# Two blocks of a model on one core: feed-forward up-projections as 512-column matmuls, and a second operator in GpSimd's multiplications

## The chip, the cores and the metric

The kernel runs on one core of a Trainium2 chip. The core has TensorE (PE in the rows, its weight loads PEld), VectorE (DVE), ScalarE (ACT), GpSimd (POOL) and SyncE (SP, which here issues every DMA). The metric is the time of one execution on the device, in microseconds (us); less is better.

## The reference

Two blocks are computed one after the other, for one sequence of 256 tokens of width 2048, all in fp32. The first has a modulation by c, a mixer (a recurrence and a pooling part) and a feed-forward with a convolution over three tokens; the second has another modulation and two attention branches. The change touches the feed-forward and the modulation:

```python
c_act = jax.nn.silu(c)
mod = c_act @ w_ada[l] + b_ada[l]          # w_ada: 2048 x 12288; the second block has its own, 2048 x 6144
...
def _conv_ffn(h, w_up, conv_w, conv_b, w_down):
    u = h @ w_up                           # 2048 -> 2 x 5632 features
    up = jnp.pad(u, ((0, 0), (CONV_WIDTH - 1, 0), (0, 0)))
    y = conv_b
    for j in range(CONV_WIDTH):
        y = y + conv_w[j] * up[:, j:j + T]
    val, gate = jnp.split(y, 2, axis=-1)
    return (jax.nn.silu(gate) * val) @ w_down
```

## The kernel before

Activations lie with features on the 128 partitions and the 256 tokens along the free dimension. Products are made to nearly fp32 from parts of fewer bits: every operand is split into a high and a low part, and three products are summed: weight high by activation high, weight high by activation low, weight low by activation high. The activations' parts of one feature tile lie side by side in `ACTS`, `AH` being the high 256 columns and `AL` the low 256.

Work comes in **units** of 1 MB of weights. For each unit SP loads the weights into one of four ring slots (`ring`), ACT copies them to the high part (`w_high`, L1337), DVE subtracts to get the low part (`w_low`, L1737), and PE multiplies. The order of units is fixed in a list, each engine runs its own written-out order, and semaphores join them. A slot is loaded again when PE has finished its unit; ACT and DVE split two units ahead.

There are two ways in which PE does a unit of 16 feature tiles. `std` makes, for each tile, two matmuls of 256 columns with the high weights into the same 256 columns of a PSUM bank (L768, L769), then 16 of 256 columns with the low weights (L772). `paired` makes one matmul of 512 columns with the high weights, over `AH` and `AL` together, into the 512 columns of the bank (L785), then the 16 with the low weights into the first half (L788). After `paired` the two halves of the bank must still be added: ACT copies the first half to SBUF and DVE adds the second half to it (`added`, L1847) and frees the bank. After `std` ACT's copy is the whole result and frees the bank.

The **feed-forward** goes through the 5632 hidden features in 11 turns of 512. Turn i has 8 up units (4 value tiles and 4 gate tiles, in turn) and then the 4 down units of the turn before it, `down(i - 1, s)`; before the change all 88 up units are done with the columns of `std` (the first three by `tiled`, tile by tile as the input becomes ready). For each up unit ACT copies the bank to `rawu` (L1539) and DVE convolves it in `conv` (L2163 to L2165); for each pair DVE multiplies gate and value (`hfu`, L2170), ACT makes the high part, and DVE the low part (`hid_low`, L2175). In a down unit DVE adds both of its banks to the running sum `dacc` (L2200). DVE's order is: split the weights of the unit two ahead, then the work on this unit; after the eighth up unit come the four down units, again each with a split ahead of it.

**GpSimd** makes part of the modulation, c times `w_ada`, beside the rest. In `quarters` a turn of 512 columns of `w_ada` comes in four quarters; for each of 16 tiles GpSimd multiplies by a column of `cact` (L623 for the first, else L625) and adds to a running sum (L626), each instruction waiting for the one before. Two turns (`acc_e`) are made at the start of the program, eleven (`acc2`) beside the eleven turns of the feed-forward, and four more (`acc_g`, L689 and L693) during the attention. PE takes up the sum of turn i - 1 at the end of turn i. SP's queue loads the quarters between the rings' weights: a quarter waits until GpSimd has finished the second last one (`f_free`, L452), and the loads behind it in the queue wait with it.

Of the kernel before, what the change touches and what calls it, by code (L numbers as in the profile page):

```python
# [17 lines left out]
ALU = mybir.AluOpType  # L18
# [3 lines left out]
T = 256  # L22
D = 2048
DT = D // P
# [105 lines left out]
def program(nc, xT_in, consts, att_consts, params, pos, w_ada, w_in, w2, a2, g2, pool_w, w_out, w_up, w_down,  # L130
            w_ada2, w_in2, w_kvb, w_mla, w_dil, w_o, out):
    ctx = ExitStack()
    with ctx:
# [469 lines left out]
        def _(pool):  # L603
# [11 lines left out]
            def quarters(k, acc, prod, first):  # L615

                for q in range(4):
                    pool.wait_ge(f_landed[k % 2], 16 * (k // 2 + 1))
                    w = (AE if k < 4 * N_FIRST else AF)[k % 2][:, :].rearrange("p (j n) -> p j n", j=4)
                    for j in range(4):  # L620
                        col = cact[:, first + 4 * q + j:first + 4 * q + j + 1]
                        if q == j == 0:
                            ins = pool.tensor_scalar(acc[:, :], w[:, j, :], col, None, ALU.mult)  # L623
                        else:
                            after(pool.tensor_scalar(prod[:, :], w[:, j, :], col, None, ALU.mult))  # L625
                            ins = pool.tensor_tensor(acc[:, :], prod[:, :], acc[:, :], ALU.add)  # L626
                        if j < 3:
                            after(ins)
                    k += 1
                    ins.then_inc(f_free, 1)  # L630
                    pool.wait_ge(f_free, k)
                pool.memset(small[:, 56:57], 0.0).then_inc(ada_sums, 1)
# [48 lines left out]
            for turn in range(N_LATE):  # L681
                acc = acc_g[turn % 2]
                if turn >= 2:
                    pool.wait_ge(ada_full, N_EARLY + 1 + N_FFN + turn - 1)
                for j in range(DT):
                    k = DT * turn + j
                    pool.wait_ge(g_landed[k % 2], 16 * (k // 2 + 1))
                    o = acc if j == 0 else prod_g[:, :].rearrange("p (a b) -> p a b", a=2)
                    pool.tensor_scalar(o, AG[k % 2][:, :].rearrange("p (a b) -> p a b", a=2), cact[:, DT + j:DT + j + 1], None,  # L689
                                       ALU.mult).then_inc(g_free, 1)  # L690
                    pool.wait_ge(g_free, k + 1)
                    if j:
                        after(pool.tensor_tensor(acc, o, acc, ALU.add))  # L693
                pool.memset(small[:, 56:57], 0.0).then_inc(ada_sums, 1)
# [10 lines left out]
        def _(pe):  # L705
# [452 lines left out]
            for i in range(12):  # L1158
                if i == 0:
                    tiled([("up", 0, k) for k in range(3)], 0)  # L1160
                    std(("up", 0, 3), 3)
                elif i < 11:
                    for k in range(4):
                        std(("up", i, k), k)
                if i < 11:
                    for k in range(4, 8):
                        std(("up", i, k), k % 4)
                if i:
                    for s in range(4):
                        down(i - 1, s)  # L1170
                    ada(acc2[(i - 1) % 2])
# [158 lines left out]
        def _(act):  # L1330
# [199 lines left out]
            for i in range(12):  # L1530
                for k in range(8):
# [4 lines left out]
                    if i < 11:  # L1536
                        unit("up", i, k)
                        act.wait_ge(raw_free, B.up("raw_free"))
                        act.activation(rawu[k % 2][:, 2:T + 2], bank[k % 4][:, 0:T], ACT.Copy)\  # L1539
                            .then_inc(bank_free[k % 4], 1)  # L1540
                    if k % 2 == 0 and (k or i):
                        finish()
                    if k == 7 and 0 < i < 10:
# [180 lines left out]
        def _(v):  # L1724
# [430 lines left out]
            ahead("up", 0, 3, to=0)  # L2155

            def conv(i, n):
                raw_tile(n % 4)
                u = rawu[n % 2]
                gate = n % 2  # L2160
                o = sil[:, :] if gate else cva[n // 2 % 2][:, :]
                k = 4 * i + n // 2 + 44 * gate
# [412 lines left out]
```

## Time and profile before

| | |
|---|---|
| time, median of 3 runs | 2772.86 us (2759.91 to 2775.61) |
| span of the profiled execution | 2768.1 us |
| busy: PE, PEld | 2643.3 us (95%), 2397.8 us (87%) |
| busy: DVE, ACT, POOL | 1864.0 (67%), 1082.6 (39%), 1128.9 us (41%) |
| chain that ended last | PE 80%, DMA 6%, POOL 6%, DVE 5% |

The span runs from the first to the last instruction of the profiled execution; its time as a run is not listed apart from that, and the median of the runs lies 4.8 us above the span. A busy share is a mean over stages with different limits, and PE's busy time is modelled: the end of a matmul overlaps the next one, so PE's pace is read from the distance between starts. The feed-forward runs from about 700 us to about 1475 us of the span.

### The profile page before, as it was taken

The numbers are of one execution on the slowest core, as the hardware profiler recorded it, in microseconds if no ns is written. First come the engines' busy times: TensorE is split into PE (matmuls) and PEld (weight loads), VectorE is DVE, ScalarE is ACT, GpSimd is POOL, SyncE is SP. The second block draws the span as 40 slices with busy tenths as digits, with TensorE's granted clock in tenths as the row PEclk, the third lists the DMA queues.
The fourth block names the chain that finished last, engine by engine and source line by source line (L and its number), as shares of the span: only waits on it lengthen the run. The fifth ranks groups of instructions, "written<-read, shape, count | busy, mean of one in ns | idle before, by whom it ended". The sixth has DMA issues, their size and how long they took to land.

```text
span 2768.1 us, 47948 instructions
## 1 busy us (share of the span) xinstructions
PE 2643.3 (95%) x20992; PEld 2397.8 (87%) x20992; DVE 1864.0 (67%) x2268; ACT 1082.6 (39%) x1255; POOL 1128.9 (41%) x612
## 2 busy tenths in 40 slices
PE   5689989999999999999999999999999999999997
PEld 2268877778999999999999899989988898999996
DVE  1248863267988888888887775576446874786454
ACT  1133422144434444343446443444334444444353
POOL 0293011013899999999991475862000000000001
PEclk7689989899999999999999999999999999999998
DMA  8967647676877777777765776775767665666664
GB/s 314 321 180 187 183 153 256 221 230 191 228 218 240 240 240 240 240 243 244 243 221 138 190 194 201 209 209 171 183 193 187 161 174 179 172 168 168 183 185 120
DMA packets 759185, 568.49 MB, mean 205 GB/s; under 512 B 46497, under 2 KB 645665, under 8 KB 758849
## 3 DMA queue, kind: packets, MB, share of 16 engines
q1 hardware_dynamic: 758976, 565.42, 69.7%
q8 instruction: 166, 2.72, 0.4%
q14 instruction: 43, 0.34, 0.0%
HBM read 563.29 MB, written 2.10 MB: 204 GB/s over the span
## 4 chain that ended last, share of the span: by engine, by line
PE 80%; DMA 6%; POOL 6%; DVE 5%; ACT 1%; issue 1%; SPq 1%; DVEq 0%; POOLq 0%
PE bank L785 15%; PE bank L768 9%; PE bank L769 9%; PE bank L772 9%; PE bank L788 8%; PE bank L752 5%; PE bank L754 5%; PE bank L753 5%; PE bank L1009 2%; DMA ada<-w_ada 2%; PE bank L741 2%; PE bank L821 2%; PE bank L822 2%; PE bank L823 2%; POOL prod_e L625 1%; POOL prod L625 1%
## 5 line engine op out<-in xcount | busy, mean ns | idle before, releaser
L1737 DVE TENSOR_TENSOR w_low<-ring,w_high 128x2048 fp32r<-128x2048 f32 x388 | 951.2, 2452 | 341.9 <-ACT w_high L1337 334.8
L1337 ACT ACTIVATE w_high<-ring 128x2048 fp32r<-128x2048 f32 x388 | 738.5, 1904 | 368.7 <-DMA ring<-w_in 127.6
L768 PE MATMUL bank<-acts,w_high 128*128 128x256 f32 x2400 | 586.4, 285 | 0.0
L769 PE MATMUL bank<-acts,w_high 128*128 128x256 f32 x2400 | 583.6, 283 | 0.0
L785 PE MATMUL bank<-acts,w_high 128*128 128x512 f32 (+1 forms) x2064 | 502.3, 396 | 11.1 <-DVE acts L1804 6.4
L768 PEld LDWEIGHTS bank<-acts,w_high 128*128 128x128 f32 x2400 | 461.6, 192 | 1.1 <-issue 0.2
L769 PEld LDWEIGHTS bank<-acts,w_high 128*128 128x128 f32 x2400 | 461.7, 192 | 0.0
L785 PEld LDWEIGHTS bank<-acts,w_high 128*128 128x128 f32 (+1 forms) x2064 | 382.7, 190 | 89.9 <-DVE acts L1804 6.5
L625 POOL TENSOR_SCALAR prod<-adf,cact 128x512 f32<-128x512 f32 x165 | 378.8, 2296 | 22.2 <-DMA adf<-w_ada 6.1
L639 POOL TENSOR_TENSOR sumf<-sqf 128x256 f32<-128x256 f32 x1 | 0.7, 743 | 789.7 <-ACT sqf L1718 789.7
L772 PE MATMUL bank<-acts,w_low 128*128 128x256 f32 x2400 | 312.4, 283 | 0.0
L626 POOL TENSOR_TENSOR acc<-prod,acc 128x512 f32<-128x512 f32 x165 | 299.0, 1812 | 13.8
L772 PEld LDWEIGHTS bank<-acts,w_low 128*128 128x128 f32 x2400 | 298.8, 192 | 0.0
L788 PEld LDWEIGHTS bank<-acts,w_low 128*128 128x128 f32 (+1 forms) x2064 | 264.1, 191 | 12.6 <-DVE w_low L1737 2.5
L788 PE MATMUL bank<-acts,w_low 128*128 128x256 f32 (+1 forms) x2064 | 268.0, 283 | 1.3 <-DVE w_low L1737 1.3
L752 PE MATMUL bank<-hid_high,w_high 128*128 128x256 f32 x704 | 201.0, 285 | 6.7 <-DVE dacc L2202 3.4
L754 PE MATMUL bank<-hid_high,w_low 128*128 128x256 f32 x704 | 200.7, 285 | 0.0
L753 PE MATMUL bank<-hid_low,w_high 128*128 128x256 f32 x704 | 200.5, 285 | 0.0
L689 POOL TENSOR_SCALAR prod_g<-adg,cact 128x512 f32<-128x512 f32 x60 | 117.0, 1951 | 92.3 <-DMA adg<-w_ada 89.2
L752 PEld LDWEIGHTS bank<-hid_high,w_high 128*128 128x128 f32 x704 | 136.7, 194 | 7.3 <-issue 4.4
L753 PEld LDWEIGHTS bank<-hid_low,w_high 128*128 128x128 f32 x704 | 136.6, 194 | 0.0
L754 PEld LDWEIGHTS bank<-hid_high,w_low 128*128 128x128 f32 x704 | 136.5, 194 | 0.0
(457 smaller groups left out, 3711.2 us busy)
## 6 DMA issues: line engine op xcount, KB each, us to landing
ring<-w_in SPq DMA_DIRECT2D x182, 1024.0 KB, 5.8
ring<-w_up SPq DMA_DIRECT2D x88, 1024.0 KB, 5.9
ada<-w_ada SPq DMA_DIRECT2D x76, 1024.0 KB, 6.2
adf<-w_ada SPq DMA_DIRECT2D x44, 1024.0 KB, 8.1
ring<-w_down SPq DMA_DIRECT2D x44, 1024.0 KB, 6.4
ring<-w_out SPq DMA_DIRECT2D x16, 1024.0 KB, 6.0
adg<-w_ada SPq DMA_DIRECT2D x64, 256.0 KB, 5.6
ring<-w_mla SPq DMA_DIRECT2D x16, 1024.0 KB, 5.5
```

The lines of the kernel that those rows point to most:

```text
L625: after(pool.tensor_scalar(prod[:, :], w[:, j, :], col, None, ALU.mult))
L626: ins = pool.tensor_tensor(acc[:, :], prod[:, :], acc[:, :], ALU.add)
L752: pe.matmul(o, wh, ah, start=first, stop=False, skip_group_check=True)
L753: pe.matmul(o, wh, al, start=False, stop=False, skip_group_check=True)
L754: return pe.matmul(o, wl, ah, start=False, stop=last, skip_group_check=True)
L768: pe.matmul(o, wh[:, j], AH[:, j, :], start=j == 0, stop=False, skip_group_check=True)
L769: pe.matmul(o, wh[:, j], AL[:, j, :], start=False, stop=False, skip_group_check=True)
L772: mm = pe.matmul(o, wl[:, j], AH[:, j, :], start=False, stop=j == 15, skip_group_check=True)
L785: pe.matmul(o, wh[:, j], both, start=j == 0, stop=False, skip_group_check=True)
L788: mm = pe.matmul(o[:, 0:T], wl[:, j], AH[:, j, :], start=False, stop=j == 15, skip_group_check=True)
L1337: act.activation(WH[s][:, 0:WIDE[n]], ring[s][:, 0:WIDE[n]], ACT.Copy).then_inc(high_done, 1)
L1737: v.tensor_tensor(WL[s][:, 0:WIDE[n]], ring[s][:, 0:WIDE[n]], f32(WH[s][:, 0:WIDE[n]]), ALU.subtract)\
```

## The change

The 85 up units that were done by `std` are done by `paired`; the first three, in `tiled`, stay. ACT still copies the first 256 columns; the bank is freed by DVE's addition of the second 256 columns to the copy, ahead of the convolution. GpSimd's multiplications by c, in the turns of 512 columns and in those of the attention stage, get a second operator, a multiplication by the constant 1.0.

```diff
@@ quarters
                         if q == j == 0:
-                            ins = pool.tensor_scalar(acc[:, :], w[:, j, :], col, None, ALU.mult)
+                            ins = pool.tensor_scalar(acc[:, :], w[:, j, :], col, 1.0, ALU.mult, ALU.mult)
                         else:
-                            after(pool.tensor_scalar(prod[:, :], w[:, j, :], col, None, ALU.mult))
+                            after(pool.tensor_scalar(prod[:, :], w[:, j, :], col, 1.0, ALU.mult, ALU.mult))
                             ins = pool.tensor_tensor(acc[:, :], prod[:, :], acc[:, :], ALU.add)
@@ the attention stage's turns
-                    pool.tensor_scalar(o, AG[k % 2][:, :].rearrange("p (a b) -> p a b", a=2), cact[:, DT + j:DT + j + 1], None,
-                                       ALU.mult).then_inc(g_free, 1)
+                    pool.tensor_scalar(o, AG[k % 2][:, :].rearrange("p (a b) -> p a b", a=2), cact[:, DT + j:DT + j + 1], 1.0,
+                                       ALU.mult, ALU.mult).then_inc(g_free, 1)
@@ PE
                     tiled([("up", 0, k) for k in range(3)], 0)
-                    std(("up", 0, 3), 3)
+                    paired(("up", 0, 3), 3)
                 elif i < 11:
                     for k in range(4):
-                        std(("up", i, k), k)
+                        paired(("up", i, k), k)
                 if i < 11:
                     for k in range(4, 8):
-                        std(("up", i, k), k % 4)
+                        paired(("up", i, k), k % 4)
@@ ACT
                         act.activation(rawu[k % 2][:, 2:T + 2], bank[k % 4][:, 0:T], ACT.Copy)\
-                            .then_inc(bank_free[k % 4], 1)
+                            .then_inc(half_taken if i or k > 2 else bank_free[k % 4], 1)
@@ DVE
             def conv(i, n):
-                raw_tile(n % 4)
                 u = rawu[n % 2]
+                if i or n > 2:
+                    added(u[:, 2:T + 2], n % 4)
+                else:
+                    raw_tile(n % 4)
                 gate = n % 2
...
             def added(o, b, rows=P):

                 v.wait_ge(half_taken, B.up("half_taken"))
                 v.tensor_tensor(o, bank[b][0:rows, T:2 * T], o, ALU.add).then_inc(bank_free[b], 1)
                 raw_tile(b)
```

On PE, in the up units of a turn of the feed-forward (`w_high_61`, `w_low_57` and so on are the ring slots' high and low parts), before, the end of one unit and the start of the next:

```order
L768 MATMUL bank<-acts,w_high_61 128x256
L769 MATMUL bank<-acts,w_high_61 128x256
L772 MATMUL bank<-acts,w_low_57 128x256 [waits low_done]
L772 MATMUL bank<-acts,w_low_57 128x256 x15
L768 MATMUL bank<-acts,w_high_58 128x256 [waits bank_free0,high_done]
L769 MATMUL bank<-acts,w_high_58 128x256
```

and after the change, one whole unit and the start of the next:

```order
L785 MATMUL bank<-acts,w_high_61 128x512 [waits bank_free3,high_done]
L785 MATMUL bank<-acts,w_high_61 128x512 x15
L788 MATMUL bank<-acts,w_low_57 128x256 [waits low_done]
L788 MATMUL bank<-acts,w_low_57 128x256 x15
L785 MATMUL bank<-acts,w_high_58 128x512 [waits bank_free0,high_done]
```

The 16 pairs of 256 columns, L768 and L769 in turn, have become 16 of 512; the order of units and what each waits for are the same, but `bank_free` now comes from DVE. On DVE, from one split of weights to the next in the same part of a turn, before (`sil` is the gate's tile, `rawu_147` the copy that ACT made):

```order
L1737 TENSOR_TENSOR w_low_57<-ring_53,w_high_61 128x2048 [waits high_done]
L2175 TENSOR_TENSOR hid_low_143<-hfu,hid_high_141 128x256 [waits act_to_dve]
L2163 TENSOR_SCALAR sil<-rawu_147,par 128x256 [waits bank_free1,dve_to_pe]
L2164 SCALAR_TENSOR_TENSOR sil<-rawu_147,par,sil 128x256 [waits dve_seq]
L2165 SCALAR_TENSOR_TENSOR sil<-rawu_147,par,sil 128x256 [waits dve_seq]
L2214 MEMSET small 128x1 [waits raw_free]
L1737 TENSOR_TENSOR w_low_54<-ring_50,w_high_58 128x2048 [waits high_done]
```

and after:

```order
L1737 TENSOR_TENSOR w_low_57<-ring_53,w_high_61 128x2048 [waits high_done]
L2178 TENSOR_TENSOR hid_low_143<-hfu,hid_high_141 128x256 [waits act_to_dve]
L1847 TENSOR_TENSOR rawu_147<-bank,rawu_147 128x256 [waits half_taken,dve_to_pe]
L2166 TENSOR_SCALAR sil<-rawu_147,par 128x256 [waits bank_free1]
L2167 SCALAR_TENSOR_TENSOR sil<-rawu_147,par,sil 128x256 [waits dve_seq]
L2168 SCALAR_TENSOR_TENSOR sil<-rawu_147,par,sil 128x256 [waits dve_seq]
L2217 MEMSET small 128x1 [waits raw_free]
L1737 TENSOR_TENSOR w_low_54<-ring_50,w_high_58 128x2048 [waits high_done]
```

One instruction is added ahead of each convolution, and the next split of weights stands one instruction later. ACT's and GpSimd's orders stay as they are.

## Rows read from the trace of the kernel before

**Rows 1.** The page: the span, and each engine's busy time with its instructions.

```profile
span 2768.1 us, 47948 instructions
PE 2643.3 (95%) x20992; PEld 2397.8 (87%) x20992; DVE 1864.0 (67%) x2268; ACT 1082.6 (39%) x1255; POOL 1128.9 (41%) x612
```

**Rows 2.** The page: shares of the span in the chain that ended last.

```profile
PE 80%; DMA 6%; POOL 6%; DVE 5%; ACT 1%; issue 1%; SPq 1%; DVEq 0%; POOLq 0%
```

**Rows 3.** One turn: length, then busy us (instructions) of PE, PEld, DVE, ACT, POOL; clock.

```profile
1032.00:1101.90 69.90, 69.90 (x585) 69.90 (x584) 59.91 (x62) 28.31 (x29) 65.39 (x33) 1.00 0.78 241
```

**Rows 4.** Timeline of ACT: start, length; copies after seven up units, first and last.

```profile
1034.86 0.39 ACT L1539 ACTIVATE rawu<-bank 128x256 f32<-128x256 f32 x1 [2.85 <-PE bank L772]
...
1069.41 0.39 ACT L1539 ACTIVATE rawu<-bank 128x256 f32<-128x256 f32 x1
```

**Rows 5.** The chain in order of time, paired units of `w_out`.

```profile
597.46 3.65 PE bank L785 x16
601.11 1.91 PE bank L788 x16
603.02 3.65 PE bank L785 x16
```

**Rows 6.** Timeline of POOL during two up units of one turn.

```profile
1051.19 3.48 POOL L625 TENSOR_SCALAR prod<-adf,cact 128x512 f32<-128x512 f32 x1
...
1057.93 2.34 POOL L626 TENSOR_TENSOR acc<-prod,acc 128x512 f32<-128x512 f32 x1
...
1063.54 3.48 POOL L625 TENSOR_SCALAR prod<-adf,cact 128x512 f32<-128x512 f32 x1
```

**Rows 7.** Timeline of DVE in the same turn: splits of weights.

```profile
1049.98 3.25 DVE L1737 TENSOR_TENSOR w_low<-ring,w_high 128x2048 fp32r<-128x2048 f32 x1
...
1056.45 2.65 DVE L1737 TENSOR_TENSOR w_low<-ring,w_high 128x2048 fp32r<-128x2048 f32 x1
...
1074.70 3.27 DVE L1737 TENSOR_TENSOR w_low<-ring,w_high 128x2048 fp32r<-128x2048 f32 x1
```

**Rows 8.** DVE's splits in the whole program: ns, shortest, median, longest.

```profile
L1737 DVE TENSOR_TENSOR w_low<-ring,w_high x388: 689/2293/3425, 106.4 to 2734.6; 128x2048 fp32r<-128x2048 f32 x193, 128x512 fp32r<-128x512 f32 x1
```

**Rows 9.** What DVE waited for in five turns (1030 to 1380 us): total, times, longest.

```profile
DVE cva L2163 <- ACT rawu L1539: 19.1, 10, 2.8
DVE dacc L2200 <- PE bank L754: 11.0, 12, 1.4
```

**Rows 10.** DVE's additions of halves elsewhere: ns, shortest, median, longest.

```profile
L1847 DVE TENSOR_TENSOR kd<-bank,kd x24: 408/422/425, 2106.7 to 2504.0; 128x256 f32<-128x256 f32 x24
L1847 DVE TENSOR_TENSOR qn<-bank,qn x16: 410/414/425, 1528.1 to 1872.4; 128x256 f32<-128x256 f32 x16
```

**Rows 11.** POOL's operations: ns, shortest, median, longest.

```profile
L625 POOL TENSOR_SCALAR prod_e<-ade,cact x30: 1562/1564/5608, 123.4 to 228.0; 128x512 f32<-128x512 f32 x30
L626 POOL TENSOR_TENSOR acc_e<-prod_e,acc_e x30: 1259/1286/3270, 125.0 to 229.7; 128x512 f32<-128x512 f32 x30
L639 POOL TENSOR_TENSOR sumf<-sqf x1: 743/743/743, 2673.2 to 2673.2; 128x256 f32<-128x256 f32 x1
```

**Rows 12.** POOL's groups in five turns (1032 to 1381 us): busy, mean ns, idle before.

```profile
L625 POOL TENSOR_SCALAR prod<-adf,cact 128x512 f32<-128x512 f32 x75 | 174.2, 2323 | 7.4
L626 POOL TENSOR_TENSOR acc<-prod,acc 128x512 f32<-128x512 f32 x75 | 137.6, 1834 | 6.3
L623 POOL TENSOR_SCALAR acc<-adf,cact 128x512 f32<-128x512 f32 x5 | 14.7, 2943 | 8.7 <-DMA adf<-w_ada 8.7
```

**Rows 13.** Two stretches: length, then busy us of PE, PEld, DVE, ACT, POOL; clock.

```profile
205.00:235.00 30.00, 28.07 (x157) 23.95 (x157) 22.67 (x28) 12.97 (x11) 25.01 (x15) 1.00 0.97 247
770.00:840.00 70.00, 63.96 (x508) 63.58 (x507) 56.27 (x62) 25.78 (x25) 65.45 (x34) 0.95 0.77 234
```

**Rows 14.** The chain in order of time: SP's queue, released by POOL, and the loads behind.

```profile
200.73 0.37 SPq L452
201.14 8.36 DMA ring<-w_in
...
785.35 0.37 SPq L452
785.76 7.68 DMA ring<-w_down
```

## The prediction

> **What bounds the kernel now.** The page comes first. PE is busy for 95% of the span [rows 1] and makes up 80% of the chain that ended last [rows 2], but both are means over stages, so the stage of the change has to be read by itself. One turn of the feed-forward in the table of stretches shows PE busy for all of its 69.9 us at full clock, GpSimd for 65.4 and DVE for 59.9 [rows 3]. PE is the bound there, and two other engines have only 4.5 and 10 us of room.
>
> PE's pace is read from the ends of units. ACT copies a bank as soon as its unit is done, and seven copies in a row start from 1034.86 to 1069.41 [rows 4]: six steps in 34.55 us, 5.76 us for a `std` unit. The units of `w_out`, which are `paired` already, stand in the chain at 3.65 and 1.91 us, and the next begins 5.56 us after the one before [rows 5]. The columns are the same 12288, so what differs is 16 matmul starts: 0.20 us.
>
> Then GpSimd and DVE, which hold each other up. A split of weights on DVE has a median of 2.29 us [rows 8], but in a turn it takes 3.25 when it starts inside an addition of GpSimd's and 2.65 when it starts inside a multiplication [rows 7]. In the other direction, a multiplication that starts under a split takes 3.48 and an addition 2.34 [rows 6], against 1.56 and 1.29 undisturbed [rows 11]. So one addition of GpSimd's costs DVE up to 3.25 - 2.29 = 0.96 us and one multiplication 0.36, together 1.3. The two settle in a pattern: the long multiplication at 1051.19 comes back at 1063.54 [rows 6], and in these 12.35 us GpSimd makes three multiplications and three additions while DVE does two up units. PE needs 2 x 5.76 = 11.52 for two. DVE therefore falls behind PE by 0.83 us with each pair of up units, and recovers in the four down units, where it waits for PE again, as it does at the start of a turn [rows 9].
>
> How much room is left at the worst place? The split for the third down unit is the last of a run that is late: it starts at 1074.70 and takes 3.27, so it is ready at 1077.97 [rows 7]. PE ended the eighth up unit just before 1069.41 [rows 4] and has two down units of the same 48 matmuls of 256 columns to do first, 11.52 us: it wants that split at 1080.9. The room is 2.9 us.
>
> **The change, part by part.** *PE:* 85 units at 0.20 us, 17 us in all; 1.6 us for each turn of eight. This is the only sure gain.
>
> The Trainium skill (TensorE: Matmul & The Clock Gate, section "Wait — 56ns, not 53.3ns?") puts the fixed cost of a warm matmul at about 2.5 ns, by which 16 fewer starts would give 0.04 us per unit and 3.4 us in all. The trace disagrees: 5.76 against 5.56. The rows decide, and the rule gets no chance of its own.
>
> *DVE:* one addition per unit, reading PSUM and SBUF. The same instruction elsewhere takes 0.41 to 0.43 us, and no longer while GpSimd works in the attention stage [rows 10]; that bounds it from both sides. With the gap to the next instruction I take 0.45, so 0.9 for a pair of units. The 3.6 us per turn do not lie on PE's path as such; they make DVE later. A pair on DVE becomes 12.35 + 0.9 = 13.25 us against PE's 11.12, so DVE falls behind by 2.13 where it was 0.83, 1.3 more for each pair. The first pair of a turn hides it in the wait at the turn's start (19.1 us in five turns, [rows 9]); over the other three pairs it is 3.9 us. The room of 2.9 takes most, and PE waits 1.0 us at the third down unit. A longer pair also holds more of GpSimd's work: at one multiplication and addition in 4.12 us it is 3.2 instead of 3, and 0.2 x 1.3 us for three pairs adds 0.8. So PE's wait is 1.0 to 1.8 us and the turn changes by -0.6 to +0.2; ten turns give -6 to +2, and the five units of turn 0 give -1. I take the upper end, because behind the late addition stand ACT's next copies (the copy of a unit waits for the convolution two before) and behind those ACT's splits, so that a late DVE delays high parts too: +2 - 1 = +1.
>
> *Banks:* `bank_free` now comes from DVE, later than from ACT. A bank is wanted again four units later, some 20 us, against a DVE lag of under 10. I cost this at nothing; it would show only after DVE's lag had passed three units.
>
> *The second operator:* no instruction of GpSimd in the trace has one. From below: an addition of 256 columns reads as many elements, 512 per partition, in 0.74 us [rows 11]. From above: twice the present price, 3.12. What speaks for neither direction alone is that an addition of 512 columns, with two inputs, takes 1.26 to 1.29 and a multiplication with one input 1.56 [rows 11]: its price is not that of the traffic, so the path that GpSimd's code takes for the operation decides, and a second operator can lengthen it or choose another one. The nearest row is the multiplication itself; I take 1.56, unchanged.
>
> The Trainium skill (GPSIMD Engine Reference, "Elementwise — side-by-side cycle accounting") says that up to two operations per element cost no more than the port's 1.03 cycles per element, which would make the second operator free. At its 1.2 GHz that would be an estimate of 0.44 us for 512 elements, where the trace has 1.56, so the rule's level does not hold here.
>
> What covers GpSimd? In five turns its multiplications, additions and the gaps ahead of them come to (174.2 + 137.6 + 14.7 + 7.4 + 6.3) / 5 = 68.0 us per turn, and it waits 8.7 / 5 = 1.7 us for the next turn's first quarter [rows 12]. The cover is 1.7 us per turn, 0.11 us for each of 16 multiplications. Beyond it GpSimd sets the turn.
>
> Where GpSimd is on the path already is seen in SP's queue: at 200.73 and at 785.35 a quarter's load had waited for GpSimd, and the chain goes on with the weights behind it [rows 14]. What PE lost there is small: 30.0 - 28.1 = 1.9 us, and 70.0 - 64.0 = 6.0 us [rows 13]. A shorter multiplication can win these 8 us and no more, since PE then sets the pace; a longer one adds to the first place in full, 24 multiplications stand ahead of it (six quarters).
>
> **Sum.** +1 us on the span of 2768.1. The median of the runs, 2772.9, lies 4.8 above the span, which I keep as what lies around it: 2774 us.
>
> **The rivals.**
>
> *GpSimd shorter, and DVE worse for it.* If the second operator takes a faster path, GpSimd fits four multiplications and additions into DVE's pair instead of three. DVE's pair is then 13.25 + 1.3 = 14.55, behind PE by 3.4 against 0.83; over three pairs 7.8 more, less the room of 2.9, less the gain of 1.6: +3.3 us per turn, 33 for ten, less 1 and less the 8 us above: 2797 us. For it: each of GpSimd's additions blocks DVE for as long as before, and a shorter multiplication only brings the next addition sooner. Against: GpSimd's total per turn is fixed, and SP hands it quarters at PE's pace. It decides from the point at which a fourth pair fits into 13.25 us.
>
> *GpSimd longer.* With 0.3 us more, 16 x 0.3 - 1.7 = 3.1 us per turn, 34 for eleven, and 24 x 0.3 = 7 at the start: 2814 us. It decides from 0.11 us more; at the bound of 3.12 us the turns would be over 20 us longer.
>
> *Both parts work.* GpSimd shorter without harm to DVE, and the addition hidden: -17 - 8, 2748 us. With GpSimd unchanged and the addition wholly hidden (its room at the third down unit being larger than I read): -17, 2756 us. For these: DVE has 10 us of idle time per turn [rows 3].
>
> **Chances.** No change as forecast 0.41 (2762 to 2786 by itself); GpSimd shorter and DVE late 0.20; GpSimd longer 0.15; both parts or PE's gain alone 0.24. What a measurement can tell from no change is about 0.5%, 14 us. Faster by more: the last, 0.24. Slower by more: the second and third nearly whole, 0.34. Within: 0.42. The range goes from 2748, the floor that PE sets, to 2812, which leaves out about half of the longer GpSimd and nothing else.
>
> **What would show it.** PE: copies of up units 5.56 us apart where DVE is in time. DVE: 85 additions of 0.42 us, splits for the third down unit ending later against the eighth copy than 8.6 us, and PE waiting for `w_low` ahead of down units, which it does nowhere in the turns now. GpSimd: the shortest multiplication tells the second operator's price; near 1.56 is my case. Its number of multiplications per DVE pair tells the first rival. I am wrong if the shortest multiplication is off 1.56 by over 0.1 us, or if PE's turn comes out below 68.5 us with no wait for splits.

## The result, and the profile after

The changed kernel takes 2825.0 us (median of 4 runs, 2819.5 to 2829.5) against 2767.3 before (median of 4, one run more than in the table above; 2759.9 to 2775.6): a ratio of 1.021, with a 95% interval of 1.0185 to 1.0243. The forecast was 2774, the range 2748 to 2812: the time lies outside it, on the slow side. The profiled execution took 2823.99 us, its span is 2822.2.

The page of the changed kernel: span, busy time, and the shares of the chain that ended last.

```profile
span 2822.2 us, 45313 instructions
...
PE 2642.6 (94%) x19632; PEld 2339.8 (83%) x19632; DVE 1945.8 (69%) x2353; ACT 1079.8 (38%) x1255; POOL 807.9 (29%) x612
...
PE 73%; DVE 14%; issue 6%; DMA 4%; ACT 2%; POOL 0%; SPq 0%; DVEq 0%; ACTq 0%; POOLq 0%
```

GpSimd is busy for 807.9 us in place of 1128.9 [rows 1], and its 6% of the chain are gone [rows 2]. Yet DVE's share of the chain rose from 5% to 14% and that of "issue" (an engine that waits for nothing the profile shows) from 1% to 6%, and PE, with less to do, is busy for as long as before.

Durations of GpSimd's multiplications and additions and of DVE's new additions in the changed kernel: ns, shortest, median, longest.

```profile
L625 POOL TENSOR_SCALAR prod<-adf,cact x165: 691/746/2869, 683.3 to 1473.9; 128x512 f32<-128x512 f32 x165
L625 POOL TENSOR_SCALAR prod_e<-ade,cact x30: 691/694/4732, 122.9 to 202.5; 128x512 f32<-128x512 f32 x30
...
L626 POOL TENSOR_TENSOR acc<-prod,acc x165: 1275/1337/3216, 684.1 to 1474.7; 128x512 f32<-128x512 f32 x165
...
L1847 DVE TENSOR_TENSOR rawu<-bank,rawu x85: 409/424/427, 716.1 to 1478.2; 128x256 f32<-128x256 f32 x85
```

The multiplication by two operators takes 0.69 us where the one by one operator took 1.56 [rows 11]. GpSimd's addition is as it was. DVE's 85 additions cost 0.42 us each, as forecast.

One turn of the feed-forward of the changed kernel in the table of stretches, columns as in [rows 3].

```profile
1073.70:1149.00 75.30, 70.49 (x457) 64.91 (x457) 67.50 (x71) 28.19 (x29) 42.73 (x31) 0.98 0.72 224
```

The turn is 75.3 us long in place of 69.9. GpSimd is busy for 42.7 of them, and it does that work nearly in one piece: its timeline shows it waiting 25 to 29 us per turn for the next turn's first quarter (26.4 in this one, from 1102.7), while PE does the later down units and the next up units. DVE's busy time went from 59.9 to 67.5.

What PE waited for in the feed-forward (700 to 1502 us): total, times, longest.

```profile
PE bank L752 <- DVE w_low L1737: 40.5, 14, 5.7
PE bank L752 <- DVE dacc L2203: 10.6, 7, 4.3
PE bank L788 <- DVE w_low L1737: 8.0, 5, 2.1
```

These are 59.1 us. The same view of before, for its feed-forward (700 to 1445 us), adds up to 6.7:

```profile
PE bank L752 <- DVE dacc L2202: 3.4, 1, 3.4
PE bank L752 <- DVE w_low L1737: 2.6, 1, 2.6
PE bank L752 <- DVE dacc L2200: 0.7, 1, 0.7
```

51 of the 59 us are down units (L752) that wait for DVE: for a split of weights (`w_low`), or for the addition to `dacc`, which frees a bank.

Timeline of GpSimd in the changed kernel: from one multiplication that is long because it starts under a split to the next such one.

```profile
1157.90 2.87 POOL L625 TENSOR_SCALAR prod<-adf,cact 128x512 f32<-128x512 f32 x1
1160.85 1.28 POOL L626 TENSOR_TENSOR acc<-prod,acc 128x512 f32<-128x512 f32 x1
...
1163.01 1.34 POOL L626 TENSOR_TENSOR acc<-prod,acc 128x512 f32<-128x512 f32 x1
...
1165.28 3.20 POOL L626 TENSOR_TENSOR acc<-prod,acc 128x512 f32<-128x512 f32 x1
...
1169.35 1.34 POOL L626 TENSOR_TENSOR acc<-prod,acc 128x512 f32<-128x512 f32 x1
...
1171.62 1.34 POOL L626 TENSOR_TENSOR acc<-prod,acc 128x512 f32<-128x512 f32 x1
1173.06 2.87 POOL L625 TENSOR_SCALAR prod<-adf,cact 128x512 f32<-128x512 f32 x1
```

In these 15.16 us there are five additions. The pattern of before held three in 12.35 us: the one shown in [rows 6] and these two.

```profile
1054.76 1.37 POOL L626 TENSOR_TENSOR acc<-prod,acc 128x512 f32<-128x512 f32 x1
...
1062.07 1.38 POOL L626 TENSOR_TENSOR acc<-prod,acc 128x512 f32<-128x512 f32 x1
```

Timeline of DVE in the changed kernel, in the same stretch: start, length.

```profile
1156.69 3.26 DVE L1737 TENSOR_TENSOR w_low<-ring,w_high 128x2048 fp32r<-128x2048 f32 x1
...
1160.78 1.51 DVE L2166 TENSOR_SCALAR sil<-rawu,par 128x256 f32<-128x256 f32 x1
1162.32 0.88 DVE L2167 SCALAR_TENSOR_TENSOR sil<-rawu,par,sil 128x256 f32<-128x256 f32 x1
1163.23 1.40 DVE L2168 SCALAR_TENSOR_TENSOR sil<-rawu,par,sil 128x256 f32<-128x256 f32 x1
```

The split takes 3.26 in place of 2.29 [rows 8], and the small steps of the convolution, 0.41 to 0.48 us where nothing disturbs them, take 1.51 and 1.40 when they meet an addition of GpSimd's. Each of these additions costs DVE 0.9 to 1.1 us, at whichever of the three kinds of instruction it meets.

Timeline of PE in the changed kernel at a turn's first down unit (the idle time before it in brackets).

```profile
1094.30 0.48 PE L752 MATMUL bank<-hid_high,w_high 128*128 128x256 f32 x1 [3.91 <-DVE w_low L1737]
...
1097.57 0.41 PE L752 MATMUL bank<-hid_high,w_high 128*128 128x256 f32 x1
...
1098.05 0.28 PE L752 MATMUL bank<-hid_high,w_high 128*128 128x256 f32 x1
```

And the table of stretches there, whose third column from the right is the granted clock.

```profile
1094.00:1096.00 2.00, 1.71 (x8) 1.71 (x9) 1.93 (x4) 0.00 (x0) 1.92 (x2) 0.61 0.41 160
1096.00:1098.00 2.00, 2.00 (x12) 2.00 (x11) 1.93 (x3) 0.00 (x0) 1.82 (x3) 0.54 0.00 0
1098.00:1100.00 2.00, 2.00 (x19) 2.00 (x19) 1.96 (x3) 1.14 (x3) 1.82 (x3) 1.00 0.04 8
```

The wait itself is 3.9 us. Behind it the granted clock is half (1.2 of 2.4 GHz) for some 3.4 us: 12 matmuls in the second of these stretches, 19 in the third. That happens once at the first two down units of each of turns 1 to 8, behind waits of 1.8 to 4.7 us, and each time loses up to 1.7 us more.

### The profile page after: what moved, and what is told of

Its sections match the earlier page's. It is cut to its first block, busy times and chain, and to the rows that moved or that the text cites. A ratio compares the mean times of both kernels' runs of the same rounds, so it can differ in the third digit from the quotient of the medians.

```text
span 2822.2 us, 45313 instructions
## 1 busy us (share of the span) xinstructions
PE 2642.6 (94%) x19632; PEld 2339.8 (83%) x19632; DVE 1945.8 (69%) x2353; ACT 1079.8 (38%) x1255; POOL 807.9 (29%) x612
## 4 chain that ended last, share of the span: by engine, by line
PE 73%; DVE 14%; issue 6%; DMA 4%; ACT 2%; POOL 0%; SPq 0%; DVEq 0%; ACTq 0%; POOLq 0%
PE bank L785 20%; PE bank L788 11%; PE bank L768 4%; PE bank L752 4%; PE bank L769 4%; PE bank L772 4%; PE bank L753 4%; PE bank L754 4%; DMA ada<-w_ada 2%; PE bank L1009 2%; PE bank L741 2%; PE bank L823 2%; PE bank L821 2%; PE bank L822 2%; DVE sil L2167 1%
## 5 line engine op out<-in xcount | busy, mean ns | idle before, releaser
L785 PE MATMUL bank<-acts,w_high 128*128 128x512 f32 x3424 | 827.8, 394 | 12.6 <-DVE acts L1804 8.6
L785 PEld LDWEIGHTS bank<-acts,w_high 128*128 128x128 f32 x3424 | 632.9, 189 | 139.5 <-DVE acts L1804 8.7
L788 PEld LDWEIGHTS bank<-acts,w_low 128*128 128x128 f32 x3424 | 438.5, 191 | 27.2 <-DVE w_low L1737 10.8
L788 PE MATMUL bank<-acts,w_low 128*128 128x256 f32 x3424 | 445.3, 283 | 8.0 <-DVE w_low L1737 8.0
L626 POOL TENSOR_TENSOR acc<-prod,acc 128x512 f32<-128x512 f32 x165 | 285.1, 1728 | 13.8
L752 PE MATMUL bank<-hid_high,w_high 128*128 128x256 f32 x704 | 209.1, 297 | 51.1 <-DVE w_low L1737 40.5
L768 PE MATMUL bank<-acts,w_high 128*128 128x256 f32 x1040 | 256.3, 286 | 0.0
L769 PE MATMUL bank<-acts,w_high 128*128 128x256 f32 x1040 | 254.2, 284 | 0.0
L768 PEld LDWEIGHTS bank<-acts,w_high 128*128 128x128 f32 x1040 | 201.0, 193 | 1.1 <-issue 0.2
L769 PEld LDWEIGHTS bank<-acts,w_high 128*128 128x128 f32 x1040 | 201.1, 193 | 0.0
L625 POOL TENSOR_SCALAR prod<-adf,cact 128x512 f32<-128x512 f32 x165 | 181.1, 1097 | 50.6 <-DMA adf<-w_ada 35.7
L752 PEld LDWEIGHTS bank<-hid_high,w_high 128*128 128x128 f32 x704 | 142.9, 203 | 55.2 <-DVE w_low L1737 43.3
L772 PE MATMUL bank<-acts,w_low 128*128 128x256 f32 x1040 | 135.4, 283 | 0.0
L772 PEld LDWEIGHTS bank<-acts,w_low 128*128 128x128 f32 x1040 | 129.5, 192 | 0.0
L741 PE MATMUL bank<-ada,c_wide 128*32 128x512 f32 x608 | 102.6, 772 | 26.1 <-DMA ada<-w_ada 22.1
```

Of the source, the lines that this page charges most:

```text
L625: after(pool.tensor_scalar(prod[:, :], w[:, j, :], col, 1.0, ALU.mult, ALU.mult))
L752: pe.matmul(o, wh, ah, start=first, stop=False, skip_group_check=True)
L768: pe.matmul(o, wh[:, j], AH[:, j, :], start=j == 0, stop=False, skip_group_check=True)
L769: pe.matmul(o, wh[:, j], AL[:, j, :], start=False, stop=False, skip_group_check=True)
L772: mm = pe.matmul(o, wl[:, j], AH[:, j, :], start=False, stop=j == 15, skip_group_check=True)
L785: pe.matmul(o, wh[:, j], both, start=j == 0, stop=False, skip_group_check=True)
```

## The experiments

Three theories stood. **One:** the shorter multiplication lets more of GpSimd's additions fall into the time in which DVE serves up units, each costs DVE about 1 us, and down units wait for late splits. **Two:** DVE's own 85 additions are the cost. **Three:** the two-operator multiplication itself holds DVE up longer.

All ratios are against the kernel before, with 95% intervals. For the table at the end, a *turn* is the distance of ACT's copies of the fifth up unit from turn 2 to turn 9, over seven; a *pair* is DVE's time from the first convolution step of an odd up unit to that of the next (second and third pair of turns 3 to 9); the *feed-forward* reaches from the start of ACT's first up copy to the start of DVE's last addition to `dacc`. The expectations give some turns and pairs by rougher readings, a few tenths off.

**One-operator multiplications, the rest as changed.**

```diff
-                            after(pool.tensor_scalar(prod[:, :], w[:, j, :], col, 1.0, ALU.mult, ALU.mult))
+                            after(pool.tensor_scalar(prod[:, :], w[:, j, :], col, None, ALU.mult))
```

(and at the two other multiplications).

> The changed kernel with GpSimd's multiplications back to one operator; the 85 paired up units and DVE's additions stay. Theory 1 (the second operator shortens the multiplication from 1.56 to 0.69 us, and the denser additions of GpSimd that follow hold DVE up): the multiplication is 1.56 us again, GpSimd gets some three multiplications and additions into DVE's pair of up units, and the time is that of before within 12 us, 2765 to 2782. Theory 2 (the 85 additions on DVE are the cost, 85 x 0.47 = 40 us and the lost time behind them): still slow, 2805 to 2820. Theory 3 (a two-operator multiplication itself holds DVE up longer than a one-operator one): as theory 1, 2765 to 2782.

Measured: 2761.3 us, 0.9993 (0.9972 to 1.0013). The table of stretches for a turn:

```profile
1038.30:1107.40 69.10, 68.75 (x457) 63.37 (x457) 61.75 (x70) 28.58 (x29) 63.74 (x33) 1.00 0.79 244
```

A pair is 12.56 us with three additions of GpSimd's. DVE's 85 additions are all there, and with PE's gain they come out at no change that can be measured: theory two falls for this form of the kernel. They are not free: PE's waits in the feed-forward are 16.4 us, against 6.7 before.

**The second operator alone.** The paired units and DVE's additions are taken back.

```diff
-                        paired(("up", i, k), k)
+                        std(("up", i, k), k)
...
-                            .then_inc(half_taken if i or k > 2 else bank_free[k % 4], 1)
+                            .then_inc(bank_free[k % 4], 1)
```

> The kernel before with the second operator alone: up units in 256-column matmuls as before, no additions on DVE. Theory 1: GpSimd's multiplication takes 0.69 us; DVE's pair of up units grows from 12.35 us to about 14 by two more GpSimd additions of about 1 us each in it, PE waits for splits ahead of down units, and the time is 2785 to 2810 (some 3 us more in each of ten turns, less about 6 us gained ahead of the feed-forward). Theory 2: no additions, so no loss, and the gain ahead of the feed-forward is kept: 2755 to 2765. Theory 3: slow like theory 1, 2785 to 2810.

Measured: 2818.7 us, 1.018 (1.0157 to 1.0212). The table of stretches for a turn:

```profile
1062.70:1138.40 75.70, 72.29 (x587) 71.71 (x586) 66.02 (x62) 28.16 (x29) 44.69 (x33) 0.98 0.72 222
```

The second operator alone makes 1.8 of the 2.1%, and that is more than theory one had put it, 2785 to 2810: a pair holds five additions and takes 15.0 us, where two more had been expected to make 14. Theory two is out.

**A memset behind each multiplication in the eleven turns of the feed-forward.**

```diff
+                            if k >= 4 * N_FIRST:
+                                after(pool.memset(idle2[:, :], 0.0))
                             ins = pool.tensor_tensor(acc[:, :], prod[:, :], acc[:, :], ALU.add)
```

> The changed kernel with one more instruction on GpSimd behind each multiplication of the feed-forward's ten later turns: a memset of a scratch tile of 128x512, whose result nobody reads. It reads nothing and only spaces GpSimd's additions out; multiplications, additions and DVE's own work stay. Theory 1: with multiplication and memset together at 1.2 to 2 us, DVE's pair of up units holds fewer additions and the turn comes back most of the way to 70 us: 2765 to 2800. Theory 2 and theory 3: nothing that they hold responsible has changed, 2815 to 2830 or more by the memset's own writes.

Measured: 2821.2 us, 1.020 (1.0178 to 1.0219): a miss for theory one as it was put. The timeline of GpSimd, additions alone:

```profile
1134.17 3.08 POOL L629 TENSOR_TENSOR acc<-prod,acc 128x512 f32<-128x512 f32 x1
...
1138.71 1.29 POOL L629 TENSOR_TENSOR acc<-prod,acc 128x512 f32<-128x512 f32 x1
...
1141.51 2.62 POOL L629 TENSOR_TENSOR acc<-prod,acc 128x512 f32<-128x512 f32 x1
...
1145.64 1.29 POOL L629 TENSOR_TENSOR acc<-prod,acc 128x512 f32<-128x512 f32 x1
...
1148.44 3.08 POOL L629 TENSOR_TENSOR acc<-prod,acc 128x512 f32<-128x512 f32 x1
```

The pattern closes after 14.27 us with four additions, one fewer than without the memset. That shortens the pair, but GpSimd is now busy for 56.3 us of a turn instead of 42.7, and PE waits no less (61.6 us in the feed-forward). The run doesn't part theories one and three.

**No additions on GpSimd.** The two-operator multiplications stay.

```diff
-                            after(pool.tensor_scalar(prod[:, :], w[:, j, :], col, 1.0, ALU.mult, ALU.mult))
-                            ins = pool.tensor_tensor(acc[:, :], prod[:, :], acc[:, :], ALU.add)
+                            ins = pool.tensor_scalar(prod[:, :], w[:, j, :], col, 1.0, ALU.mult, ALU.mult)
+                            if k < 4 * N_FIRST or j < 3:
+                                after(ins)
+                            if k < 4 * N_FIRST:
+                                ins = pool.tensor_tensor(acc[:, :], prod[:, :], acc[:, :], ALU.add)
```

> The changed kernel without GpSimd's additions in the feed-forward's turns; the two-operator multiplications and DVE's 85 additions stay. It leaves out the sums over those modulation columns, so that the last partial product stands for them. Theory 1: what holds DVE up is gone, DVE's pair of up units falls to 12 us or less, and PE runs at the paired pace: 2740 to 2765. Theory 2: DVE's additions are still there: 2805 to 2825. Theory 3: the multiplications still hold DVE up: 2800 to 2825.

Measured: 2729.6 us, 0.987 (0.9849 to 0.9892). The table of stretches for a turn, and two steps of DVE's timeline, the second under a multiplication:

```profile
1026.00:1094.40 68.40, 68.40 (x457) 63.27 (x456) 53.31 (x69) 28.27 (x28) 18.52 (x17) 1.00 0.79 245
```

```profile
1027.29 0.48 DVE L2170 SCALAR_TENSOR_TENSOR cva<-rawu,par,cva 128x256 f32<-128x256 f32 x1
...
1032.92 0.81 DVE L2170 SCALAR_TENSOR_TENSOR sil<-rawu,par,sil 128x256 f32<-128x256 f32 x1
```

PE is never idle and runs at the paired pace. A two-operator multiplication costs DVE 0.33 us here, as the one-operator one did (0.36, from [rows 7]); theory three falls. That the time is below the expected 2740 has a reason in the kernel before: its feed-forward, too, pays for GpSimd's additions (742.9 us, against 732.5 with `std` units and no additions, below).

**Two memsets.**

```diff
                                 after(pool.memset(idle2[:, :], 0.0))
+                                after(pool.memset(idle2[:, :], 0.0))
```

> As the run with one memset behind each of GpSimd's multiplications in the feed-forward, but with two (0.53 us each). In the runs so far DVE's pair of up units took 12.8 us with three GpSimd additions in it (one-operator multiplications), 14.0 with four (one memset), 15.2 with five (the changed kernel). Theory 1 in this form (the number of additions that fall into a pair sets DVE's pace, 1.2 us each, and the spacing sets their number): one multiplication, two memsets and one addition need at least 0.7 + 1.1 + 1.3 + 0.4 of gaps = 3.5 us, stretched to some 4.2 by DVE, so three additions per pair, a pair near 13 us and 2760 to 2790. Theory 3 (the two-operator multiplication holds DVE up by itself): no better than with one memset, 2815 or more.

Measured: 2781.2 us, 1.006 (1.0036 to 1.0079), as theory one had it: three additions in a pair, 13.00 us. GpSimd does more work here than in the changed kernel, and the whole is 1.5% faster.

**The same work, later.** Only SP's order differs. `quarter(i, q)` loads the quarter that GpSimd works on next.

```diff
-                ups(i, (0, 1))
+                ups(i, (0,))
+                if i > 1:
+                    quarter(i - 1, 2)
+                ups(i, (1,))
                 if i == 1:
                     quarter(0, 3)
-                ups(i, (2, 3))
+                ups(i, (2, 3, 4))
+                if i > 1:
+                    quarter(i - 1, 3)
+                ups(i, (5, 6, 7))
+                downs(i - 1, (0,))
                 quarter(i, 0)
-                ups(i, (4, 5))
+                downs(i - 1, (1, 2))
                 quarter(i, 1)
-                ups(i, (6, 7))
-                quarter(i, 2)
-                downs(i - 1, (0, 1))
-                quarter(i, 3)
-                downs(i - 1, (2, 3))
-            downs(10, range(4))
+                downs(i - 1, (3,))
+            quarter(10, 2)
+            downs(10, (0, 1))
+            quarter(10, 3)
+            downs(10, (2, 3))
```

> The changed kernel with SP's order alone changed: the loads of a modulation quarter stand later in each turn (behind the first and third down load and behind the next turn's first and fifth up load, in place of behind the fourth, sixth and eighth up load and the second down load), so that GpSimd's additions spread over the down units too, where DVE has room. Additions, multiplications and DVE's work are the same in number. Theory 1: fewer additions in DVE's pairs of up units, turns of 69 to 70 us in place of 75, and the first load no longer waits for GpSimd at the feed-forward's entry: 2740 to 2770. Theory 2 (DVE's own additions) and theory 3 (the multiplication holds DVE up, wherever it falls in the up phase): the turn stays near 75 us, 2805 to 2830.

Measured: 2758.6 us, 0.9973 (0.9958 to 0.9989). The table of stretches for a turn:

```profile
1037.30:1106.60 69.30, 68.78 (x458) 63.39 (x457) 60.93 (x70) 28.36 (x29) 46.53 (x32) 1.00 0.79 243
```

No instruction was taken out, and 66 us of the changed kernel are gone. Of a turn's 15 additions seven now fall into the three pairs of up units (three, one and three), in place of 12 to 15; six begin while PE does down units, in place of three or four, and there DVE has room.

**One-operator multiplications in the feed-forward's turns alone.**

```diff
+                            if k < 4 * N_FIRST:
+                                after(pool.tensor_scalar(prod[:, :], w[:, j, :], col, 1.0, ALU.mult, ALU.mult))
+                            else:
+                                after(pool.tensor_scalar(prod[:, :], w[:, j, :], col, None, ALU.mult))
```

> The changed kernel with one-operator multiplications in the feed-forward's turns alone; before it (two turns) and behind it (the attention rows) they keep the second operator, and the up units stay paired. Theory 1: the feed-forward is that of the run with one-operator multiplications (69.1 us per turn), and GpSimd's first two turns end some 25 us sooner, of which PE's wait at the entry bounds the gain: 2748 to 2762, 0 to 13 us under that run. If the second operator costs elsewhere too, it is slower than that run, above 2765.

Measured: 2763.0 us, 0.9992 (0.9978 to 1.0006): the ratio of the first run, and 1 us above the expected range. GpSimd ends its first two turns at 204.1 us where that run has 229.8. PE is busy for 98.8 us of the stretch from 120 to 235 us instead of 96.2, but nothing of that is left in the time. In its profiled execution the turn is 70.0 us and the feed-forward 746.0, against 69.3 and 739.9 in the first run, where the same had been expected.

**The later order with one operator.** SP's order as in the edit above, and, at all three multiplications:

```diff
-                            after(pool.tensor_scalar(prod[:, :], w[:, j, :], col, 1.0, ALU.mult, ALU.mult))
+                            after(pool.tensor_scalar(prod[:, :], w[:, j, :], col, None, ALU.mult))
```

> The later order of SP's quarter loads with one-operator multiplications everywhere and paired up units: it tells what the order gives without the second operator. Theory 1: a one-operator turn of GpSimd fills some 65 us wherever its loads stand, so DVE's pair still holds three additions: 68.5 to 70 us per turn, 2750 to 2768, no faster than the late order with two operators by more than 5 us. If the order itself is what decides, both late kernels come out alike, within 5 us.

Measured: 2763.7 us, 0.9989 (0.9973 to 1.0004), 5 us from the two-operator version. With 7.6 additions in the three pairs the turn is 68.7 us: the order reaches nearly the same turn from either multiplication. The feed-forward is 729.3 us, 10.6 shorter than in the first run, but the program isn't: behind it PE now waits 4.3 us for `sqy` and 3.8 for `xT`, waits that the first run doesn't have.

**PE's term by itself.** No additions on GpSimd, and:

```diff
-                        paired(("up", i, k), k)
+                        std(("up", i, k), k)
```

> The kernel before with two-operator multiplications and without GpSimd's additions in the feed-forward's turns (it leaves out the sums over those modulation columns, as the run with paired units did). Beside that run, at 2729.6 us, it measures PE's own term with nothing late: if 16 fewer matmul starts are worth 0.20 us per unit, 85 units make 17 us, so 2745 to 2749. If the paired units gain nothing for PE, 2728 to 2732.

Measured: 2749.0 us, 0.9942 (0.9921 to 0.9963), 19.4 us over the paired run. The table of stretches for a turn:

```profile
1037.10:1107.10 70.00, 70.00 (x587) 70.00 (x586) 49.89 (x61) 28.38 (x28) 17.78 (x17) 1.00 0.78 240
```

In both runs the turn is PE alone, without a wait in the whole feed-forward: a pair of up units takes 11.52 us here and 11.13 in the paired run, 0.195 us per unit, 16.6 us for 85.

**The later order without the paired units.** SP's later order with two operators, and the same edit to `std`.

> The later order of SP's quarter loads with two operators, but the up units as before (256-column matmuls, no additions on DVE). Against the run with the same order and paired units, at 2758.6 us, it tells what the first part of the change is worth where GpSimd's additions are spread. If the order hides DVE's additions, up to 17 us slower, 2762 to 2776; if pairing still costs as much as it gains, within 6 us, 2753 to 2764; if DVE's additions are still a cost, faster, under 2752.

Measured: 2760.4 us, 0.9982 (0.9967 to 0.9998). The turn is 70.0 us, PE's floor for `std` units; with paired units in the same order it was 69.15, 0.7 over theirs. The total is the same within 2 us, as it should be if pairing costs as much as it gains: this order does not bring out what pairing could give.

**Later still.** The quarters are loaded behind the down units 2 and 3 and behind the up units 3 and 7 of the next turn; those lines of SP's loop now read (the last turns' loads are written out behind it):

```python
                ups(i, (2, 3))
                if i > 1:
                    quarter(i - 1, 2)
                ups(i, (4, 5, 6, 7))
                if i > 1:
                    quarter(i - 1, 3)
                if i < 10:
                    downs(i - 1, (0, 1, 2))
                    quarter(i, 0)
                    downs(i - 1, (3,))
                    quarter(i, 1)
```

> The changed kernel with the quarter loads spread further: behind the third and fourth down load and behind the next turn's fourth and eighth up load. In the first later order two of three pairs of up units still held three GpSimd additions each (13.0 to 13.2 us) and one held one (10.3). With quarters two to five units apart the pairs should hold two to three (11.4 to 13.0), the turn 68 to 69.4 us against 69.4: 2742 to 2760. If the spread within the up units doesn't matter beyond what the first later order gave, within 4 us of 2758.6.

Measured: 2750.5 us, 0.9941 (0.9921 to 0.9961). The table of stretches for a turn:

```profile
1037.10:1105.60 68.50, 68.50 (x458) 63.30 (x457) 60.18 (x70) 28.21 (x28) 49.62 (x32) 1.00 0.79 246
```

PE is busy throughout this turn, at the length of the run without GpSimd's additions. The pairs are not the even ones that were expected: three, one and three additions, or three, none and four. This version is ahead of both kernels, by 0.6% and by 2.6%, with the change kept whole.

What the runs show together (us):

| Kernel | additions of GpSimd in a pair | pair | turn | feed-forward |
|---|---|---|---|---|
| `std`, none | 0 | 11.52 | 70.01 | 732.5 |
| paired, none | 0 | 11.13 | 68.49 | 716.4 |
| before (`std`, one operator) | 3 | 12.36 | 70.01 | 742.9 |
| paired, one operator | 3 | 12.56 | 69.31 | 739.9 |
| paired, two operators, two memsets | 3 | 13.00 | 71.30 | 764.7 |
| paired, two operators, one memset | 4 | 14.28 | 75.80 | 804.9 |
| `std`, two operators | 5 | 14.97 | 75.26 | 795.9 |
| changed (paired, two operators) | 5 | 15.1 | 75.24 | 800.0 |
| paired, two operators only in the first two turns | 3 | 12.59 | 69.99 | 746.0 |
| `std`, two operators, later order | 3, 1, 3 | 13.1, 10.0, 13.6 | 70.01 | 734.7 |
| paired, one operator, later order | 3, 3, 2 or 3, 2, 2 | 12.6, 12.6, 11.4 or 12.6, 11.2, 11.4 | 68.74 | 729.3 |
| changed, later order | 3, 1, 3 | 13.2, 10.3, 13.0 | 69.15 | 735.0 |
| changed, later still | 3, 1, 3 or 3, 0, 4 | 12.3, 10.6, 12.3 or 12.3, 9.2, 13.8 | 68.49 | 724.5 |

With the loads in their old order the second and third pairs of a kernel all hold the same number of additions: the pattern of the two engines repeats with each pair, as the timelines show. One addition more, with its multiplication, makes a pair 1.3 us longer (12.56 to 15.1 in two steps, 13.00 to 14.28 in one). The pair alone does not give the turn: with one memset it is shorter than in the changed kernel, and the turn no better; the two later orders have seven additions in three pairs alike, and differ by 0.7 us per turn.

## Why the prediction was wrong

**The step that failed** is "I take 1.56, unchanged" for the second operator. The price is 0.69 us, below even the 0.74 taken as the bound from below. With it the forecast's branch of no change was left, and the first rival came true. The price alone does not explain the miss: by the prediction's own working for a shorter multiplication the time would have been 2797, inside the range.

**That rival had the mechanism and was sized too small:** 2797 forecast, 2825 measured. It put four additions into a pair of 14.55 us and 3.3 us onto a turn. The profile shows five in 15.1, and 75.24 - 70.01 = 5.2 us per turn. Ten times the missing 1.9 us are 19 of the 34 between the rival's +24 and the measured +58 (the kernel before came out at 2767.3, not at 2772.9); the rest lies outside the steady turns, 8 of it a gain that the rival took off. The price of a multiplication with its addition, 1.3 us, was right; their number was not: with 0.69 us instead of an unnamed shorter time, a fifth fits in, and the pair is some 0.55 us longer than worked out. The clock behind a wait was not in the sum at all: the records of the granted clock show 44.4 us of half clock in the feed-forward against 6.8 before; 3.8 of the 44.4 fall into waits, so that is up to 16.9 us more. And the 8 us that a shorter multiplication should win at the two places of [rows 13] weren't won. At 205 to 235 us PE has no wait left, but the run with two operators in the first two turns alone has the ratio of the one without. At 770 to 840 us PE is busy for 61.3 of the 70 us, where before it was 64.0: the 6.0 us have become 8.7. What speaks against the rival, "SP hands it quarters at PE's pace", was wrong in effect: the loads come within six units, so a faster GpSimd does most of its work beside up units and rests beside most of the down units, where it does less harm.

The sum for the feed-forward: 59.1 - 6.7 = 52.4 us more of waits, up to (44.4 - 3.8 - 6.8) / 2 = 16.9 by the clock, less 16.6 by the pairing, 53 of the 57 us by which it grew (742.9 to 800.0).

**The place and the wait:** the room for the split of the third down unit was the wrong one to watch. In the changed kernel the longest wait of most turns is at the first, 3.9 us at 1094.30. The third waits too, but for a bank that DVE's addition to `dacc` frees, not for a split:

```profile
1108.46 0.36 PE L752 MATMUL bank<-hid_high,w_high 128*128 128x256 f32 x1 [0.90 <-DVE dacc L2203]
```

So it is in every run in which the third down unit of a steady turn waits (0.3 to 1.2 us in the run with one operator, 1.8 with the second operator alone). That wait has no term in the prediction. Its "nowhere in the turns now", of PE waiting for `w_low`, holds for turns 1 to 9 of the kernel before; the first down unit of turn 0 waits 2.6 us for a split.

**PE's gain** was right: 0.20 us per unit and 17 in all forecast, 0.195 and 16.6 measured. The Trainium skill's fixed cost per matmul (TensorE: Matmul & The Clock Gate, "Wait — 56ns, not 53.3ns?"), by which 3.4 us would be gained, does not hold here: 0.195 us for 16 starts is 12 ns for each.

**DVE's additions** were right in size (0.42 us) and in what they come to: the forecast had them eat PE's gain to +1 us, and the kernel with that part alone runs at 0.9993; its turn is 0.7 us shorter, just beyond the lower end of the forecast's -0.6 to +0.2, and its feed-forward 3 us. In part that is luck, as its wait at the third down unit is the one for the bank.

**Banks** of up units cost nothing, as said: in no run, the changed kernel included, does an up unit wait for one.

**The Trainium skill's rule on operators** (GPSIMD Engine Reference, "Elementwise — side-by-side cycle accounting"), that two per element cost no more than one, had been set aside for its level. The trace now agrees that a second one adds nothing, and not with the level: it takes 0.87 us off, and 0.69 us is above the estimate of 0.44 worked out from that page.

What stays open: why the form with one operator takes 1.56 us. The runs show both prices, and nothing of what lies behind them.

## What to carry to other kernels

An engine off the critical path that gets faster isn't always harmless: ask where its work will then fall, and whom it blocks there. Where two engines hold each other up, count the blocking instructions per period of the slower one, and move their loads into the stretch where it has room before taking anything out. A price that no row of the trace shows deserves a chance on either side, and the branch with the larger consequence deserves the working.

## What the hardware showed that was not expected

- GpSimd multiplies 128x512 f32 by a column in 1.56 us with one operator and in 0.69 us with two, the second being times 1.0. The addition of two such tiles is 1.26 to 1.28 us at its shortest in either kernel.
- An addition of GpSimd's costs a DVE instruction that meets it about 1 us at each of three lengths: 0.41 becomes 1.51, 0.48 becomes 1.40, 2.29 becomes 3.26 us. DVE's addition out of PSUM (`rawu<-bank,rawu`) stays at 0.41 to 0.43 us in all 85 cases.
- Behind waits of 1.8 to 4.7 us PE was granted half its clock for about 3.4 us, in each of turns 1 to 8; behind some waits of 1.8 us in the run with the second operator alone it kept its clock. In turns 2 to 8 of the later orders, where it waits under 1 us, the granted clock is 1.00.
- With the loads in their old order the second and third pairs of a turn hold the same number of additions: one memset of 0.53 us takes it from five to four, a second one to three.
